# Feed-forward stages of two streams: one 512-column matmul for both in place of two of 256 columns

## The reference

```
for l in range(DEPTH):                       # DEPTH = 2
    mod_x, mod_c = ada_params(c, w_ada[l], b_ada[l]), ada_params(c_ctx, w_ada[l], b_ada[l])
    x     = swiglu_half_step(x,     g[l, 0], mod_x, 0, w_ffn_up[l, 0], w_ffn_down[l, 0])
    h_ctx = swiglu_half_step(h_ctx, g[l, 0], mod_c, 0, w_ffn_up[l, 0], w_ffn_down[l, 0])
    ... attention of both over w_in[l], w_out[l] ...
    x     = swiglu_half_step(x,     g[l, 2], mod_x, 6, w_ffn_up[l, 1], w_ffn_down[l, 1])
    if not last:
        h_ctx = swiglu_half_step(h_ctx, g[l, 2], mod_c, 6, w_ffn_up[l, 1], w_ffn_down[l, 1])

def swiglu_half_step(x, g, mod, j, w_up, w_down):
    h = modulate(rms_norm(x, g), mod[j], mod[j + 1])
    gt, up = split(h @ w_up, 2)              # 1024 -> 2 x 2816
    return x + 0.5 * mod[j + 2] * ((silu(gt) * up) @ w_down)
```

## Time and profile before

| | |
|---|---|
| three runs | 2552.15, 2554.95 and 2566.07 us, median 2554.95 |
| profiled execution | 2549.3 us from first to last instruction; it has no other time of its own |
| busy | PE 94%, its weight loads 91%, DVE 65%, ACT 39% of the span |
| matmuls | 20452 recorded |
| mean granted clock | 0.966 of full speed |
| memory traffic | 352.78 MB, mean 138 GB/s |

### The profile page before, as it was taken

The page is one execution under the profiler, slowest core; times in us unless marked ns, Lnnn a source line. Parts: engine busy times, 40 slices in busy tenths (PEclk is TensorE's granted clock), DMA queues, the critical chain, the costliest instruction groups (busy, mean ns, idle before and its releaser), DMA issues. The chain is left out here.

```text
span 2549.3 us, 47682 instructions
## 1 busy us (share of the span) xinstructions
PE 2391.4 (94%) x20452; PEld 2322.8 (91%) x20452; DVE 1661.0 (65%) x2777; ACT 997.7 (39%) x1468; POOL 188.2 (7%) x300
## 2 busy tenths in 40 slices
PE   7989998899799999999788999998999998988999
PEld 7889997899799999899558999998999998967999
DVE  6789888788877777744775677776333336376554
ACT  6455664465432222322473222223222223145543
POOL 0000000370000000011000900000000000100000
PEclk9899998999899999999898999999999999999999
DMA  6246652456445555412001455552222222211454
GB/s 256 95 157 226 221 190 92 144 197 237 141 143 191 188 182 187 169 59 79 14 1 67 164 190 189 186 198 91 92 96 96 100 100 96 70 52 67 162 194 157
DMA packets 104306, 352.78 MB, mean 138 GB/s; under 512 B 18976, under 2 KB 19232, under 8 KB 103840
## 3 DMA queue, kind: packets, MB, share of 16 engines
q1 hardware_dynamic: 95904, 348.94, 38.9%
q0 software_dynamic: 8192, 0.80, 0.3%
HBM read 348.63 MB, written 1.05 MB: 137 GB/s over the span
## 5 line engine op out<-in xcount | busy, mean ns | idle before, releaser
L1456 ACT ACTIVATE W_hi<-W_raw 128x1024 fp32r<-128x1024 f32 x510 | 538.7, 1060 | 1119.6 <-PE slot L930 1053.9
L1830 DVE TENSOR_TENSOR W_lo<-W_raw,W_hi 128x1024 fp32r<-128x1024 f32 x510 | 621.5, 1222 | 473.8 <-ACT W_hi L1456 465.1
L928 PE MATMUL slot<-H_hiA,W_lo 128*128 128x256 f32 x2768 | 790.9, 286 | 18.0 <-DVE H_loA L1960 4.6
L929 PE MATMUL slot<-H_loA,W_hi 128*128 128x256 f32 x2768 | 781.5, 282 | 0.0
L930 PE MATMUL slot<-H_hiA,W_hi 128*128 128x256 f32 x2768 | 780.9, 282 | 0.0
L928 PEld LDWEIGHTS slot<-H_hiA,W_lo 128*128 128x128 f32 x2768 | 533.3, 193 | 29.5 <-issue 21.1
L929 PEld LDWEIGHTS slot<-H_loA,W_hi 128*128 128x128 f32 x2768 | 535.8, 194 | 0.1
L930 PEld LDWEIGHTS slot<-H_hiA,W_hi 128*128 128x128 f32 x2768 | 532.7, 192 | 0.0
L1842 DVE SCALAR_TENSOR_TENSOR PROD<-A_raw,SC 128x1024 bf16<-128x1024 f32 x288 | 341.2, 1222 | 170.3 <-DMA A_raw<-adastream 169.8
L928 PE MATMUL slot<-H_hiB,W_lo 128*128 128x256 f32 x1376 | 385.9, 280 | 3.0 <-DVE VB L2347 1.3
L929 PE MATMUL slot<-H_loB,W_hi 128*128 128x256 f32 x1376 | 383.9, 279 | 0.0
(11 more groups left out here) (277 smaller groups left out, 3057.8 us busy)
## 6 DMA issues: line engine op xcount, KB each, us to landing
W_raw<-wstream SPq DMA_DIRECT2D x510, 512.0 KB, 3.3
A_raw<-adastream SPq DMA_DIRECT2D x144, 512.0 KB, 4.3
BT<-par POOLq DMA_DIRECT2D x256, 3.0 KB, 2.6
XA<-xT SPq DMA_DIRECT2D x2, 512.0 KB, 4.5
SC<-cond SPq DMA_DIRECT2D x1, 1024.0 KB, 14.4
XB<-ctxT SPq DMA_DIRECT2D x1, 1024.0 KB, 16.4
CON<-const SPq DMA_DIRECT2D x1, 960.5 KB, 9.6
PAR<-par SPq DMA_DIRECT2D x1, 680.0 KB, 10.8
```

The lines of the kernel that those rows point to most:

```text
L928: pe.matmul(out, wl, xh, start=start, stop=False, skip_group_check=True)
L929: pe.matmul(out, wh, xl, start=False, stop=False, skip_group_check=True)
L1456: act.activation(W_hi[:, g % HIGH, :], W_raw[:, g % RAW, :], ACT.Copy).then_inc(S.w_hi, 1)
L1830: dve.tensor_tensor(W_lo[:, g % RAW, :], W_raw[:, g % RAW, :], W_hi[:, g % HIGH, :].bitcast(F32), ALU.subtract).then_inc(S.w_lo, 1)
```

## The change

In the three joint stages a unit is no longer visited once for A and once for B. The first 3 units (`LEAD`) and the last 5 (`TAIL`) of a stage still are. The 58 between are one visit, whose matmuls take the tokens of both streams as 512 moving columns, with one weight load. The activations of the two streams stand in one tensor (`HJ`, `HIDJ`, `HFJ`), so that a tile of both is addressed as two runs of 256 columns, 16 KB apart for `HJ` and 52 KB for `HIDJ`. In PSUM one bank now holds one tile of both streams, and a token is four banks, so there are two joint tokens in turn (`shared`). ACT and DVE handle a pair of both streams with one instruction of 1024 columns in place of two of 512. The update of A and B comes in one step (`update_both`). The ada steps of these stages are 48, 24 and 48, spread evenly over the joint visits.

```diff
@@ make_streams, ffn
+        if blk == 2 and not solo:
+            stages[s][-1].place = 1 if s == "A" else None
+            if s == "A":
+                st = add(s, "ffnj", steps, solo, dict(tok=PAIRS + 2 * len(GROUPS), pair=PAIRS), l=l, blk=blk, ffn=which)
...
+                st = add(s, "ffnb", steps[:LEAD] + steps[-TAIL:], solo, dict(tok=1), l=l, blk=blk, ffn=which, mate=mate)
@@ place_ada
+    shares = {(0, 0): 2 * 3 * KT, (0, 1): 3 * KT, (1, 0): 2 * 3 * KT}
...
-        elif st.kind == "ffn" and st.blk == 2:
-            v.ada = int(left > 4)
@@ PSUM
-        slots = [ctx.enter_context(nc.psum_tensor(f"slot{i}", [P, 2, 512], F32)) for i in range(4)]
+        banks = ctx.enter_context(nc.psum_tensor("banks", [P, 8, 512], F32))
+        slots = [banks[:, 2 * i:2 * i + 2, :] for i in range(4)]
...
+        def shared(st, n):
+            h = 4 * ((st.side + n) % 2)
+            return banks[:, h:h + 4, :]
@@ tensor
+            def joined(out, wl, wh, lo, hi, start, stop):
+                out = out.rearrange("p (s n) -> p s n", s=2)
+                pe.matmul(out, wl, hi, start=start, stop=False, skip_group_check=True)
+                pe.matmul(out, wh, lo, start=False, stop=False, skip_group_check=True)
+                return pe.matmul(out, wh, hi, start=False, stop=stop, skip_group_check=True)
...
+            def up_both(st, n, q):
+                wl, wh = weights()
+                p = shared(st, n)
+                for t in range(2):
+                    for k in range(4):
+                        kt = 4 * (q % 2) + k
+                        c = slice(256 * k + P * t, 256 * k + P * t + P)
+                        mm = joined(p[:, 2 * (q // 2) + t, :], wl[:, c], wh[:, c], HJ[:, :, 1, kt, :],
+                                    HJ[:, :, 0, kt, :], kt == 0, kt == 7)
+                mm.then_inc(A.sem.done, 1)
@@ vector
+            def update_both(st, gate, n, m, done):
+                dve.wait_ge(A.sem.done, done)
+                dve.wait_ge(A.sem.evac, st.tok + n)
+                p = shared(st, n)
+                for s in (A, B):
+                    b = p[:, :, SEQ * s.half:SEQ * s.half + SEQ]
+                    update_half(s, b, gate, m, 0)
+                    a = update_half(s, b, gate, m, 1)
+                a.then_inc(A.sem.evac, 1)
```

More of the change, by code:

```diff
@@ L167, with __init__ @@
 class Old:
-    def __init__(self, s, ring, tok, gate):
-        self.s, self.ring, self.tok, self.gate = s, ring, tok, gate
+    def __init__(self, s, ring, tok, gate, side=0, place=None, both=None):
+        self.s, self.ring, self.tok, self.gate, self.side, self.place, self.both = s, ring, tok, gate, side, place, both
 G = None
@@ L190, in make_streams @@
     mode = dict(A=None, B=None)
+    side = dict(A=0, B=1)
+    both = {}
     def add(s, kind, steps, solo, more, **kw):
@@ L196, in add @@
         ring = 4 if solo and not mixing else 2
-        st = Stage(s, kind, steps, c, solo, ring, mode[s] is not None and mode[s] != ring, **kw)
+        st = Stage(s, kind, steps, c, solo, ring, mode[s] is not None and mode[s] != ring,
+                   side=side[s], **kw)
         mode[s] = ring
@@ L248, in out2 @@
         add(s, "out2", [o + u for u in OUT_UNITS], solo, dict(tok=2), l=l)
-        return Old(s, 4 if solo else 2, count[s]["tok"] - 1, (l, 1))
+        return Old(s, 4 if solo else 2, count[s]["tok"] - 1, (l, 1), side[s])
     old = None
@@ L377, in place_ada @@
     t = 0
+    shares = {(0, 0): 2 * 3 * KT, (0, 1): 3 * KT, (1, 0): 2 * 3 * KT}
+    free = {k: [v for v in ORDER if v.stage.kind == "ffnj" and (v.stage.l, v.stage.ffn) == k and v.final] for k in shares}
+    for k, n in shares.items():
+        for i, v in enumerate(free[k]):
+            v.ada = (i + 1) * n // len(free[k]) - i * n // len(free[k])
     for v in ORDER:
@@ L1008, in norm_sums @@
             def norm_sums(s, st):
+                if st.old is not None and st.old.both is not None:
+                    pe.wait_ge(A.sem.evac, st.old.both + (s is B))
+                if st.place is not None:
+                    wait(pe, s.sem.evac, norm_token(st))
                 open_token(s, st, norm_token(st))
@@ new lines, in hidden, with down_both @@
+            def hidden(j, low, k):
+                o = 2 * SEQ * (2 * j + low) + SEQ * k
+                return HIDJ[:, :, o:o + SEQ]
+            def down_both(st, n, j, first, last):
+                wl, wh = weights()
+                p = shared(st, n)
+                for k in range(2):
+                    for t in range(4):
+                        c = slice(512 * k + P * t, 512 * k + P * t + P)
+                        mm = joined(p[:, t, :], wl[:, c], wh[:, c], hidden(j, 1, k), hidden(j, 0, k),
+                                    first and k == 0, last and k == 1)
+                mm.then_inc(A.sem.done, 1)
@@ new lines, in down_part @@
+            def down_part(s, st, old, j, first, last):
+                wl, wh = weights()
+                out = blocks(old, old.tok)
+                for k in range(2):
+                    for t in range(4):
+                        c = slice(512 * k + P * t, 512 * k + P * t + P)
+                        x = slice(SEQ * k, SEQ * k + SEQ)
+                        mm = three(out[:, t, :], wl[:, c], wh[:, c], s.HID[:, j, 1, x], s.HID[:, j, 0, x],
+                                   first and k == 0 and t % 2 == 0, last and k == 1)
+                mm.then_inc(s.sem.done, 1)
@@ L1076, in out_units, with ffnb @@
+            def ffnb(s, st):
+                for q in range(LEAD):
+                    up_part(B, st.mate, q, False)
+                    yield
+                for j in range(TAIL):
+                    down_part(B, st, st.end, j, j == 0, j == TAIL - 1)
+                    yield
             def out_units(s, st, tok, qs, h_need):
```

164 lines of the change are left out of this document (143 added, 21 removed).

## The result

The changed kernel takes 2571.67 us (median of 20 runs, 2562.3 to 2583.09) against 2552.55 us (20 runs, 2538.93 to 2573.63) of the kernel before. The ratio is 1.0069, with a 95% interval of 1.0046 to 1.0091: **slower by 0.7%**, where 2494 us, 2.4% faster than the 2554.95 us known then, was predicted; it is outside the predicted range of 2476 to 2520 us. The profiled execution of the changed kernel has a span of 2567.6 us, 18.3 us more than that of before.

The account below looks back on a forecast made before the run. PE bounds the joint stages, in one of two pitches. 59.4 us saved on 4176 matmul pairs, all else priced at nothing, took the 2549.3 us span to 2489.9; moved to the median, less one, 2494 us, range 2476 to 2520.

Parts of the forecast that it names:

- the price of a 512-column matmul: PE's joint stages: 217 ns for each of 4176 matmuls replacing pairs of mean 231.2 ns, saving 59 us.
- The row that it rested on: Earlier trace of fp32 256-column matmuls: two more halves with loads add 0.21 to 0.22 us, like 512 columns.
- The half clock: At 1.2 GHz 256 columns take 213 ns with nothing added; used against a pitch by column.
- The upper bound: Joint matmul price with today's friction fixed for each load: 220 ns, or 224.5 in the slower pitch.
- the pitch is by column: Rival: weights and moving columns share memory reads, 512 columns cost twice 113.2 to 117.8 ns; 2549 to 2556 us; chance 0.05.
- the exposed load: Rival: joint matmul's next load waits for the second run, exposing up to 111 ns, +388 us, 2943 us; chance 0.05.
- The point from which it decides: Joint matmul pitch of 231 ns, 15 ns exposed, from which the exposed load decides; over 234 measurably slower.
- The rule that was weighed: The skill's back-to-back matmul gap, N/2.4 + 2.5 ns: 215.8 ns at 512 columns, a saving of 64 us.
- the 1 us that the prediction took off: Taken from the median forecast, 2495.5 to 2494 us, since a median run may have more of the slower pitch.
- the moved updates: `update_both` on DVE: eight operations in a row, 3.3 us ahead of the next split; nothing waits.
- the ends of the stages: Four ends stay about 51 us each, 9 to 10 us of PE idle; no stall, priced at nothing.
- The last doubt of the prediction: Last one-stream stage, at 113.3 ns, may change pitch; at 117.8 it would lose 6 us.

Follow-up runs that it names:

- r9: Changed kernel with five other kinds of joint matmuls (packed bf16, fp32r reading one column, bf16 4 bytes apart, 32 weight columns, plain fp32), one half stage left unchanged: 3036.73 us.
- r7: Changed kernel with joint matmuls of fewer columns, 128, 192, 320, 384, 448 and 480 in the six half stages (product incomplete): 2343.26 us.
- r1: The kernel before, unchanged, profiled once more: 2578.5 us (the other run beside it 2554.47).
- r11: r5 with the first five joint units of each stage kept at 512 columns (120 wide matmuls): 2543.04 us against 2549.90 before, ratio 0.9967.
- r10: r5 with the first nine joint units of each stage kept at 512 columns (216 wide matmuls): 2542.09 us against 2549.86 before, ratio 0.9982.
- r12: The changed kernel once more, on the same chip and beside the same runs of before as r11: 2569.39 us, ratio 1.0083 to before.
- r3: Changed kernel with each joint matmul split into two of 256 columns, each of two runs of 128 and with its own load: 2553.18 us.
- r5: Changed kernel with the joint product computed by 256-column matmuls, the rest of the change kept: 2550.58 us against 2548.36 before, ratio 1.0011.
- r6: r5 with the first joint unit of each stage wide (24 matmuls) and single extra 512-column matmuls in one-stream stages: 2545.15 us against 2548.36 before, ratio 0.9989.
- r2: Changed kernel whose joint matmuls read 512 columns of one stream in one run instead of two runs of 256: 2570.39 us.
- r4: Changed kernel whose joint matmuls read their 512 columns in four runs of 128: 2567.73 us.

## Why the prediction was wrong

**The step that failed** is the price of a 512-column matmul: "I take 217, near the row", with bounds of 216 and 224.5. It is 233.3 ns, above both. The term 4176 x (231.2 - 217) = 59 us was mis-sized, and with 233.3 it has the other sign: 8.4 us lost against the profile of before. The row that it rested on the earlier trace rows was of plain fp32, two cycles a column, and `r9` shows that such a matmul gives no sign of the limit: it adds 2.5 ns to 427, as it added 1 or 2 to 107 there. The nearest row by duration was not the nearest by rate of reading. The half clock misled in the same way: that nothing is added at 1.2 GHz was taken to speak against a cost by column; with `r9` it reads as a slower reader that is not held up.

**The upper bound was no bound.** It took the friction as a fixed sum for each load. `r7` shows it growing with the columns, 6.7 or 11.1 at 256, 13.3 at 320, 20.0 at 512. The rival that came nearest is the one given 0.05, *the pitch is by column*, twice 113.2 to 117.8 ns, which holds 233.3, with "reads of the same memory" as its reason and 2549 to 2556 us as its time; but its reason is only half right, since weights have little or no part in it (231.1 with 32 columns of them, 215.8 with all 128 when the moving columns are one), and its price took no account of the draw between two pitches. The sign was given 0.05, with another mechanism, the exposed load; that did not happen: the load lies under the matmul as before. The point from which it decides was right, though: 231 ns to break even, and 233.3 is beyond it.

**The rule that was weighed**, the Trainium skill's N/2.4 + 2.5 ("TensorE: Matmul & The Clock Gate", Back-to-back issue gap), which that section gives for an isolated matmul, beside some 131 ns at 512 columns for a stream of loads and matmuls that no run here comes near, holds to 0.1 ns for bf16, and for fp32r that reads one column (215.8), and not for fp32r that reads 512 (233.3). By it the change saves 64 us on the pairs of this profile; it costs 8.

**The two pitches** were seen in the trace of before, and their shares were taken as given by the place. They are drawn anew (`r1`). The change takes the joint stages out of this draw: it trades pairs of 226.7 or 235.6 ns for 233.3. Against an execution with all joint stages at 113.3 it costs 4176 x 6.67 = 27.8 us, against one with all at 117.8 it gains 9.3. It is slower on average as long as less than three quarters of before's joint pairs are in the slower pitch. With a share of 0.27 it would cost 17.8 us, `r11` would gain 7.6 and `r10` 5.7; measured are 17.6, 8.4 and 4.6 (from 1.0069, 0.9967 and 0.9982; the medians alone give 19.1, 6.9 and 7.8), and 21.2 in `r12`. So one share fits them roughly, an inference from the times; the five profiles at hand (before, `r1`, `r3`, `r5`, `r6`) show 0.41, which is too few to contradict it. The spread of the runs fits too: 35 us before, 21 us after. If the share is about 0.27, the 1 us that the prediction took off, because a median run may have had more of the slower pitch, went the wrong way: the profile had 0.52 (2187 of 4176).

**What held.** DVE, ACT, the moved updates, the ada steps, the rate of the DMA and the ends of the stages were priced at nothing, and `r5` measures their sum at 1.0011 (0.9975 to 1.0047). The ends take 51, 51, 50 and 52 us with 8 to 10 us of PE idle. DVE stands at 65 to 66% in the first and third stage, where 78% was worked out: the unit takes 24 x 233.3 = 5.6 us and not 5.2, and the work was less than 4.0 us, 3.7. The last doubt of the prediction, that the last stage may fall to 117.8 and lose 6 us, came true in the profile (7.0); in `r12` it was at 113.3 again, so it belongs to the draw and not to the change.

**What stays open.** What decides between 113.3 and 117.8 ns at a wait, and whether a wide stretch brings the faster one. It followed 120 and more wide matmuls in the 18 stretches counted above, but not the 588 of `r9`; the order of the intervals fits every case and is not explained. How the extra time comes about inside the reading of the columns is open as well: `r9` shows which property has it, not its mechanism.

## What to carry to other kernels

Price a new matmul shape from a row with the same bytes from column to column at the same clock; a row of the same duration with another rate of reading says nothing, and where there is none, let the range reach to the cost by column. Wider matmuls save weight loads only where the loads are not hidden already: here 256 columns hid them, and all that was left to win were 6.7 to 11.1 ns each, 13.3 to 22.2 for a pair, and the one matmul of 512 columns that replaces the pair adds 20. Before putting a term on the pitch of one profile, look at a second execution of the same kernel: what seemed to be a property of a stage was a draw.

## What the runs showed of the hardware

- From 256 columns on, fp32r columns at the 2.4 GHz level take 0.44 to 0.46 ns each, not 0.417: 146.7 ns at 320, 174.7 at 384, 202.7 at 448, 220.0 at 480, 233.3 at 512, in one run of memory, two or four alike. The extra time is gone when all columns read one address (215.8), for packed bf16 (215.8 at 512, 109.2 at 256), for plain fp32 (2.5 ns on 426.7) and at the 1.2 GHz level (213 for 256 columns). It appears for bf16 with 4 bytes between columns (113.3 at 256).
- fp32r matmuls of 256 columns with a load each run at 113.3 or at 117.8 ns. The pitch holds for hundreds of microseconds, is drawn anew at waits, and would make 4.4 ns x 17500 matmuls, 3% of this kernel, if all were drawn one way or the other. After 120 or more 512-column matmuls it was 113.3 in 18 of 18 cases of after, `r2`, `r4`, `r10`, `r11` and `r12`, and 117.8 after 588 of them in `r9`.
- In `r7`, 128-column fp32r matmuls, one behind the other but for two pauses of 0.7 and 1.9 us between starts at 755 and 758 us, went to the 1.2 GHz level at about 761 us. They stayed there with no further pause, at a pitch of 213 ns, until about 876 us; from 873 us on they were 192 columns wide. The pitch of 128 columns at the upper level was 112 ns. A window of `r7`:

```profile
760.00:900.00 140.00, 139.16 (x749) 138.99 (x749) 114.42 (x166) 42.55 (x42) 0.00 (x0) 0.59 0.60 215
```

Timeline of `r7` in that stretch, the starts 213 ns apart:

```profile
799.93 0.41 PE L1126 MATMUL banks<-HJ,W_hi 128*128 128x128 f32 x1
800.14 0.41 PE L1127 MATMUL banks<-HJ,W_hi 128*128 128x128 f32 x1
```
